# Moving the modulation loads of a two-block transformer kernel around its latent-projection stage

## The reference, cut to what matters

```
mod = silu(c) @ w_ada + b_ada                 # one vector of 12288; c is one row, w_ada is 2048 x 12288
sh1, sc1, gt1, sh2, sc2, gt2 = split(mod, 6)  # six vectors of 2048
h = rms_norm(x, g_norm1) * (1 + sc1) + sh1
q_d, k_d, v_d, cq, ckv, k_pe = split(h @ w_in)         # differential attention, and the latents
a_out = differential_attention(...)                    # 8 heads
q_m = rms_norm(cq) @ w_q_b ; kv = rms_norm(ckv) @ w_kv_b   # the latent projections
b_out = latent_attention(...)                          # 8 heads
x = x + gt1 * (concat(a_out, b_out) @ w_out)
h2 = rms_norm(x, g_norm2) * (1 + sc2) + sh2
x = x + gt2 * ((silu(h2 @ w_gate) * (h2 @ w_up)) @ w_down)
```

## Time and profile before

| | us |
|---|---|
| median of 3 runs (2666.29 to 2670.49) | 2669.9 |
| the profiled execution | 2669.1 |
| its span, first to last instruction | 2667.0 |
| TensorE busy | 2594.2 (97%) |
| VectorE busy | 1547.3 (58%) |
| ScalarE busy | 1164.6 (44%) |

### The profile page before, as it was taken

One profiled execution on the slowest core, in us unless ns is written; L12 is line 12 of the kernel. 1 busy time (PEld: TensorE's weight loads), 2 busy tenths in 40 slices (PEclk: granted clock), 3 DMA queues, 4 the chain that ended last, 5 costly groups with the idle time before them and its releaser, 6 DMA issues.

```text
span 2667.0 us, 32922 instructions
## 1 busy us (share of the span) xinstructions
PE 2594.2 (97%) x12142; PEld 2084.7 (78%) x12142; DVE 1547.3 (58%) x1700; ACT 1164.6 (44%) x1522; POOL 53.9 (2%) x86
## 2 busy tenths in 40 slices
PE   6999989899999999999999999999999999999997
PEld 2667757688888888887888888888888888888886
DVE  1456754567776555557655454556555555555555
ACT  2344554343434444443544455444444444444443
POOL 1010110000000000000000000000000000000000
PEclk8999989999999999999999999999999999999999
DMA  9967776657777655555655545566565555555652
GB/s 391 381 232 288 261 252 220 223 171 244 243 244 245 192 190 189 189 190 189 206 189 189 174 158 166 196 201 226 188 200 189 190 188 189 189 189 188 190 188 100
DMA packets 262881, 561.72 MB, mean 211 GB/s; under 512 B 9250, under 2 KB 13556, under 8 KB 261900
## 3 DMA queue, kind: packets, MB, share of 16 engines
q1 hardware_dynamic: 260688, 549.25, 61.2%
q0 software_dynamic: 1728, 9.19, 1.0%
q10 hardware_dynamic: 380, 2.13, 0.2%
HBM read 556.32 MB, written 4.21 MB: 210 GB/s over the span
## 4 chain that ended last, share of the span: by engine, by line
PE 83%; DVE 2%; ACT 1%; issue 1%; DMA 0%; POOL 0%; DVEq 0%; POOLq 0%; ACTq 0%
PE acc L633 78%; PE bank L716 2%; PE bank L663 1%; DVE w_lo L1678 0%; PE acc L857 0%; PE acc L909 0%; PE acc L855 0%; PE bank L728 0%; PE bank L866 0%; DMA raw<-in_w_ada 0%; PE bank L690 0%; DVE wide L2194 0%; DVE x_res L2198 0%; PE acc L1068 0%; PE acc L1069 0%
## 5 line engine op out<-in xcount | busy, mean ns | idle before, releaser
L1678 DVE TENSOR_TENSOR w_lo<-raw,w_hi 128x1024 fp32r<-128x1024 f32 x852 | 1037.7, 1224 | 827.5 <-ACT w_hi L1154 798.6
L1154 ACT ACTIVATE w_hi<-raw 128x1024 fp32r<-128x1024 f32 x852 | 901.0, 1060 | 1065.1 <-PE acc L633 953.8
L633 PE MATMUL acc<-w_hi,actT_hi 128*128 128x512 f32 (+1 forms) x2112 | 833.6, 395 | 1.2 <-DVE actT_lo L1813 0.8
L633 PE MATMUL acc<-w_hi,actT_lo 128*128 128x512 f32 (+1 forms) x2112 | 821.2, 389 | 0.0
L633 PE MATMUL acc<-w_lo,actT_hi 128*128 128x512 f32 (+1 forms) x2112 | 820.8, 389 | 0.0
L633 PE MATMUL acc<-w_hi,mixT_hi 128*128 128x512 f32 (+1 forms) x1280 | 504.3, 394 | 9.1 <-DVE mixT_lo L1803 4.3
L633 PE MATMUL acc<-w_hi,mixT_lo 128*128 128x512 f32 (+1 forms) x1280 | 498.0, 389 | 0.0
L633 PE MATMUL acc<-w_lo,mixT_hi 128*128 128x512 f32 (+1 forms) x1280 | 497.6, 389 | 0.0
L633 PEld LDWEIGHTS acc<-w_hi,actT_hi 128*128 128x128 f32 x2112 | 397.3, 188 | 106.5 <-issue 21.9
L633 PEld LDWEIGHTS acc<-w_hi,actT_lo 128*128 128x128 f32 x2112 | 397.1, 188 | 83.0
L633 PEld LDWEIGHTS acc<-w_lo,actT_hi 128*128 128x128 f32 x2112 | 397.7, 188 | 79.3 <-issue 1.2
(11 more groups left out here) (272 smaller groups left out, 1049.1 us busy)
## 6 DMA issues: line engine op xcount, KB each, us to landing
raw<-in_w_ff SPq DMA_DIRECT2D x128, 1024.0 KB, 5.1
raw<-in_w_in SPq DMA_DIRECT2D x108, 1024.0 KB, 5.2
raw<-in_w_ada SPq DMA_DIRECT2D x64, 1024.0 KB, 5.2
raw<-in_w_gate SPq DMA_DIRECT2D x44, 1024.0 KB, 5.1
raw<-in_w_up SPq DMA_DIRECT2D x44, 1024.0 KB, 5.2
raw<-in_w_down SPq DMA_DIRECT2D x44, 1024.0 KB, 5.1
early_mix<-in_w_ada SPq DMA_DIRECT2D x16, 1024.0 KB, 9.5
wide<-in_w_ada SPq DMA_DIRECT2D x16, 1024.0 KB, 8.8
```

The costliest lines, as they stand in the source:

```text
L633: last_mm = pe.matmul(acc[p][:, t, 0:width], act[x][:, k0 + c, t * P:(t + 1) * P], w[:, u % SPL, c * NW:c * NW + width], start=first and c ...
L1154: act.activation(w_hi[:, u % SPL, :], raw[:, ld % RAW, (u % DU) * 1024:(u % DU + 1) * 1024], ACT.Copy) \
L1678: dve.tensor_tensor(w_lo[:, u % SPL, :], raw[:, ld % RAW, (u % DU) * 1024:(u % DU + 1) * 1024], w_hi[:, u % SPL, :].bitcast(F32), ALU.subt ...
```

## The change

It does five things.

1. The 24 pairs of a loads stand elsewhere. Before: behind w loads 13, 15, 16, 18, 20, 21, 23, 24, 26, 28, 29, 31, 33, 34, 36, 37, 39, 41, 42, 44, 46, 47, 49, 50. After: behind 12 to 14, 16 to 18, 20 to 22, 24 to 26, 28 to 30, and then 38 to 40, 42 to 44, 46 to 48. None is left behind w loads 31 to 37.
2. The rows of gt1 and gt2 are made from `part` directly: a product with ones (gt2) or with the selector `sel` (gt1) sums over the partitions and spreads at once. The columns of gt1 and gt2 and their biases in `cols2` are gone; a row takes two banks.
3. The biases of gt1 and gt2 are loaded into `grow` by GpSimd (1 MB each), and VectorE adds the sums to them.
4. VectorE makes `w_lo` of unit 0 before the columns of group 1, and that of unit 1 after `modulated(0)`.
5. The part of a load 17 moves from the prologue to behind unit 0.

```diff
+PAIRS_AT = [12 + i for i in range(19) if i % 4 != 3] + [38 + i for i in range(13) if i % 4 != 3][:9]
+GAPS = [2 * (i in PAIRS_AT) for i in range(54)]
-GAPS = [0] * 12 + [2 * ((i + 1) * 24 // 39 - i * 24 // 39) for i in range(39)] + [0] * 3
...
-    return steps + [("part", LEAD), ("part", LEAD + 1)]
+    return steps + [("part", LEAD)]
...
-        return [LEAD + 1 + v] if 0 < v < NPRO - LEAD - 1 else []
-    events = [("row", n) for a in products(u - 3) for n in completed(a) if n >= len(GROUPS)]
-    events += [("columns", n) for a in products(u - 2) for n in completed(a)]
+        return [LEAD + 1 + v] if 0 <= v < NPRO - LEAD - 1 else []
+    events = [("row" if n >= len(PROLOGUE) + 4 else "columns", n) for a in products(u - 2) for n in completed(a)]
...
 # TensorE
-            def part_row(n_, kind=GT2, g=0):
-                pe.wait_ge(mod_ready, L.value("groups", n_ + 1))
-                b, _ = wait_bank()
-                for j in range(4):
-                    col = mcol[:, kind, 4 * g + j:4 * g + j + 1]
-                    ins = pe.matmul(bank[b][:, j * P:(j + 1) * P], col.broadcast_to([P, P]), ident, start=True,
-                                    stop=True)
-                ins.then_inc(bank_full[b], 1)
+            def part_row(n_):
+                pe.wait_ge(part_ready, L.value("groups", sums_of(n_), 4))
+                for j in range(2):
+                    b, _ = wait_bank()
+                    if n_ < len(GROUPS):
+                        pe.matmul(bank[b][:, :], sel[:, j:j + 1].broadcast_to([P, P]), part[:, :], start=True,
+                                  stop=True).then_inc(bank_full[b], 1)
+                    else:
+                        pe.matmul(bank[b][:, 0:S], ones[:, :], part[:, j * S:(j + 1) * S], start=True,
+                                  stop=True).then_inc(bank_full[b], 1)
...
 # GpSimd
             pool.wait_ge(o_ready, H)
+            pool.dma_start(grow, b_ada("gt1").partition_broadcast(P)).then_inc(gt1_bias, 16)
             pool.dma_start(bf[:, :], A["b_f_2"][0, :].partition_broadcast(P)).then_inc(bf_in, 16)
...
             inv_rms(D, TT)
+            pool.wait_ge(xg_ready, 4)
+            pool.dma_start(grow, b_ada("gt2").partition_broadcast(P)).then_inc(gt2_bias, 16)
...
 # VectorE
+            def part_row(n_):
+                for j in range(2):
+                    b = next_bank()
+                    if n_ < len(GROUPS):
+                        dve.wait_ge(gt1_bias, 16)
+                        at_ = (2 * (n_ - len(PROLOGUE) - 4) + j) * NW
+                        dst, sums = grow[:, at_:at_ + NW], bank[b][:, :]
+                    else:
+                        dve.wait_ge(gt2_bias, 16)
+                        dst, sums = grow[:, bass.ds(j * S if L.i is None else L.i * NW + j * S, S)], bank[b][:, 0:S]
+                    link(dve.tensor_tensor(dst, sums, dst, ALU.add))
                     dve.sem_inc(bank_free[b], 1)
...
             for s in prologue():
+                if s == ("columns", 1):
+                    split()
                 if s[0] in todo_of:
                     todo_of[s[0]](*s[1:])
-            for _ in range(DU):
-                split()
             modulated(0)
-            for _ in range(AHEAD - DU):
+            for _ in range(AHEAD - 1):
                 split()
```

More of the change, by code:

```diff
@@ L44 @@
                                ("sh2", 16))),
-                      (ROWS2, (("sc2", 16), ("gt1", 16), ("gt2", 16), ("gmix", 16), ("gmlp", 16), ("convw", 24),
+                      (ROWS2, (("sc2", 16), ("gmix", 16), ("gmlp", 16), ("convw", 24),
                                ("gq", 1), ("gk", 1), ("gqn", 1), ("gkn", 1)))):
@@ L151, in banks_of @@
 def banks_of(u):
-    return len([1 for e in modulation(u) if takes_bank(*e)])
+    return sum(2 if what == "row" else 1 for what, n_ in modulation(u) if takes_bank(what, n_))
 def pieces_of(n_):
@@ L352, in build @@
         gt_in = sem("gt_in")
+        gt1_bias = sem("gt1_bias")
+        gt2_bias = sem("gt2_bias")
         gt_used = sem("gt_used")
@@ L682, in part_columns @@
                 ins.then_inc(bank_full[b], 1)
-            def part_row(n_, kind=GT2, g=0):
-                pe.wait_ge(mod_ready, L.value("groups", n_ + 1))
-                b, _ = wait_bank()
-                for j in range(4):
-                    col = mcol[:, kind, 4 * g + j:4 * g + j + 1]
-                    ins = pe.matmul(bank[b][:, j * P:(j + 1) * P], col.broadcast_to([P, P]), ident, start=True,
-                                    stop=True)
-                ins.then_inc(bank_full[b], 1)
-            def gt1_row(g):
-                part_row(GROUPS.index((PARTS.index("gt1"), 8 * (g // 2), 8)), PARTS.index("gt1"), g)
+            def part_row(n_):
[8 more added lines that the diff above has]
+                                  stop=True).then_inc(bank_full[b], 1)
             stages = {}
@@ L927, in _ @@
             for g in range(4):
[L928 to L931, removed]
+                at = {j: lambda j=j: run(heads_at(16 + j)) for j in range(3)} if g == 0 else None
                 group(g % 2, MIXT, 8, k0=8, at=at, ready=(lambda j: outputs_taken(H + UC * j)) if g == 0 else None)
@@ L1410, in _ @@
                 if g == 0:
-                    at = {0: lambda: run(heads_at(16)), 1: lambda: [run(heads_at(17)), skip_banks(1)],
-                          2: lambda: run(heads_at(18))}
+                    at = {j: lambda j=j: run(heads_at(16 + j)) for j in range(3)}
                 else:
-                    at = {0: lambda g=g: group_sums(g - 1), 1: lambda: skip_banks(1)}
+                    at = {0: lambda g=g: group_sums(g - 1)}
                 units(4, at)
@@ L1612, in _ @@
             b_ada = lambda name: A["b_ada"][0, PARTS.index(name) * D:(PARTS.index(name) + 1) * D]
-            for name, src in (("sc2", b_ada("sc2")), ("gt1", b_ada("gt1")), ("gt2", b_ada("gt2")),
-                              ("gmix", A["g_mix_2"][0, :]), ("gmlp", A["g_mlp_2"][0, :]),
+            for name, src in (("sc2", b_ada("sc2")), ("gmix", A["g_mix_2"][0, :]), ("gmlp", A["g_mlp_2"][0, :]),
                               ("convw", A["conv_w_2"][0, :, :].rearrange("j n -> (j n)"))):
@@ L1739, in part_columns @@
                 b = next_bank()
[L1740 to L1749, removed]
-                    else:
-                        link(dve.tensor_tensor(dst, sums, bias, ALU.add))
+                kind, k0, width = GROUPS[n_]
@@ new lines, in part_columns @@
+                name = PARTS[kind]
+                cols, rows_ = (cols1, ROWS1) if name in ROWS1 else (cols2, ROWS2)
+                at_ = lambda base: slice(base + k0, base + k0 + width)
+                dst, sums, bias = mcol[:, kind, at_(0)], bank[b][:, 0:width], cols[:, at_(rows_[name][0])]
+                if width == 8:
+                    link(dve.tensor_tensor(dst.rearrange("p (h j) -> p h j", h=2),
+                                           sums.rearrange("p (j h) -> p h j", h=2),
+                                           bias.rearrange("p (h j) -> p h j", h=2), ALU.add))
+                else:
+                    link(dve.tensor_tensor(dst, sums, bias, ALU.add))
@@ new lines, in part_columns @@
+                dve.sem_inc(bank_free[b], 1)
+                if name in ("sc1", "sc2"):
+                    link(dve.scalar_tensor_tensor(out=dst, in0=dst, scalar=1.0,
+                                                  in1=cols1[:, at_(ROWS1["g" + name[2]][0])], op0=ALU.add,
+                                                  op1=ALU.mult))
+                dve.sem_inc(mod_ready, 1)
+            def part_row(n_):
[5 more added lines that the diff above has]
+                        dst, sums = grow[:, at_:at_ + NW], bank[b][:, :]
+                    else:
+                        dve.wait_ge(gt2_bias, 16)
+                        dst, sums = grow[:, bass.ds(j * S if L.i is None else L.i * NW + j * S, S)], bank[b][:, 0:S]
+                    link(dve.tensor_tensor(dst, sums, dst, ALU.add))
@@ L1752, in part_columns @@
                     dve.sem_inc(bank_free[b], 1)
[L1753 to L1772, removed]
             def units(n, at=None):
@@ L2129, in _ @@
             for g in range(4):
[L2130 to L2134, removed]
+                units(4, {j: lambda j=j: run(heads_at(16 + j)) for j in range(3)} if g == 0 else None)
                 if g == 0:
```

## The result

The changed kernel took 2677.2 us (median of 9 runs, 2674.72 to 2686.7) against 2668.9 for the kernel before (9 runs). The ratio is 1.0037, 95% interval 1.0027 to 1.0046: slower by about 10 us, where 2.05 us faster (2667.9) was forecast and 2675 was the upper end of the range. The profiled execution took 2680.65 us, 3.5 above the median of the nine; its span is 2678.2 us, 11.2 more than before, so what its profile shows of waits is somewhat more than a median execution has.

The account below looks back on a forecast made before the run. TensorE, busy 97% of the span, was taken as the bound; 7.4 + 1.9 + 3.5 - 0.95 - 9 - 0.3 + 0.5 - 1.8 - 3.3 = -2.05 us gave 2667.9 us as median, range 2660 to 2675.

Parts of the forecast that it names:

- What the stage gives back: Latent projections, 304 to 349 us: without four pairs and a columns step, 9 us saved, at most 11.8.
- -0.3 and +0.5: 349 to 376 us: pair behind unit 72 gone, -0.3 us; new pair behind unit 74 replacing a columns step, +0.5 us.
- floor of 33.2 us: Stage from 304 to 349 us: VectorE's remaining work, under which the stage can't fall.
- weak end: Smallest gain of the stage, 5.8 us: 2.8 us where TensorE is full, plus one bank wait of 2.96 us.
- Their waits: Six more neighbouring pairs before the latent projections, second a loads late by 0.59 us each: +3.5 us, between 1.0 and 6.7.
- third rival: Triples pile up: a pair's sum holds a bank, 2.96 us in each of five triples, +14.8, 2682.7 us; chance 0.17.
- the rows: Rows of gt1 and gt2 by products with ones: columns steps go, -1.8 us and -3.3 us.
- the start: Unit 0 begins near 59.7 instead of 61.80 us, unit 1 stays near 65.8; taken as 0 (0.9 possible).
- `w_out`: Last pair stands behind unit 94, before the second half's neighbour wait: -0.95 us, 0 if the wait only moves.
- upper end: The sum of the terms at their slow ends, given as +8.0 us.
- the first rival: Stage gives back all: falls to 33.2 us, neighbours wait 0.16; sum -8.3 us, 2661.6 us; chance 0.30.
- the second (the start): Start is worth unit 0's gain, 2.1 us, if something other than that load holds unit 1: 2665.8 us; chance 0.10.

Follow-up runs that it names:

- e3: The kernel before with only the new places of the pairs; ratio 1.0042, 2678.0 us.
- e4: Changed kernel, but the first a load of each pair frees its ring slot when TensorE has read it; ratio 1.0023, 2672.8 us.
- e5: Changed kernel, but pairs behind the 11 old w loads up to 29, then behind 38 to 50 without a gap; ratio 1.0011, 2670.3 us.
- e1: Changed kernel with the 24 pairs back at their old places; ratio 0.9979, 2662.8 us.
- e2: Changed kernel with the start as before (a load 17 in the prologue, both splits before modulated(0)); ratio 1.0033, 2676.6 us.
- e7: Old places, rows and start as changed; pairs behind w loads 31 to 37 make one of four products per a load; ratio 0.9979, 2661.3 us.
- e8: Changed kernel with the exponentials of the differential heads one unit later; ratio 1.0022, 2674.0 us.

## Why the prediction was wrong

**What the stage gives back** is the step that failed. It said -9 us between 304 and 349, and -0.3 and +0.5 behind it, 8.8 in all. The profile after has -3.4 (from the start of unit 60 to that of unit 72) and +0.8, so 2.6; that of e3, with the same places, -4.8 and -0.3, so 5.2. Its premise was half right: the `w_q_b` loads did stop being late, and VectorE's sum did stop holding the bank, though other steps of VectorE held it, up to 2.4 us. The wrong half was to take VectorE's idle time for a result of the late loads, of which 2.3 us would stay of 8.8: 9.4 stayed. I had read who released each wait, but not asked what would be next: with the loads in time, ScalarE waited for VectorE's maxima instead (3.4 us before, 9.6 after), and `w_hi` behind it. The floor of 33.2 us was never near. Even the weak end, 5.8, counted TensorE's work as if the clock stayed, and the pair behind unit 74 took 3.64 us where 1.9 was counted.

**Their waits** was the second miss: +3.5 us forecast, with 6.7 as its end, 12 in the profile after and 8 in e3's. I had priced neighbours singly, from pairs with a gap in front of them. In a triple the third pair meets a ring that is already behind; the longest waits, 2.22 and 2.46 us, fell on third pairs of a triple (units 50 and 58). The reason given, the release, was a part of it (e4: 2.2 us less waiting than e3); the 2.22 us at unit 50 were one late part of a load. The sum had no term for a bank that comes late (1.5 us) nor for the clock that idle time costs (3.5 us). The third rival's threshold, 1.5 us a triple, was crossed at (12 - 3.5) / 5 = 1.7 in this profile, but not in e3's, (8.3 - 3.5) / 5 = 1.0; and what there was were late a loads and one bank wait, not five bank waits of 3 us. So "slower" came true, but not by this rival's mechanism. Alone this miss makes -2.05 + 8.5 = +6.5 us, the stage's alone -2.05 + 6.2 = +4.2, both +12.7; the profiles differ by 11.2, and the terms that came out a little better make up the rest.

**Right:** 1.85 us a pair where TensorE is full (from unit 60 to unit 61 the kernel before takes 4.86 us and e5, without a pair there, 3.01); the rows (5.6 measured at the old places, 5.1 forecast, though e1's interval allows 3 to 8); the start, where unit 0 came at 59.63 and unit 1 at 65.99, held by ScalarE's third `w_hi`; both bias loads hidden, with no wait of VectorE for either. `w_out` gave 2.3 where the terms said 1.8. The upper end adds up to 7.9, not 8.0.

One rule looked borne out and was not. The Trainium skill, DMA: Bandwidth & Descriptors, Specifications, puts one core's share of HBM at about 358 GB/s, which would have put up to 5 us on the triples. The trace after shows 401 GB/s over 63 us again, and e4 took out part of the triples' waits while moving more bytes per second. So the extra time was not a limit at 358, though it came in the same place.

**The cases:** the first rival (all given back) fell with e5 and with the stage's time in all six profiles with no pairs behind w loads 31 to 37, the second (the start) with unit 1's start at 65.99; e2 agrees.

**Open:** why taking four pairs and two columns steps out of the stage shortens it by only some 1 us, 3 at most. The lower clock takes part of it and the ring of waits the rest; no run separates them, and e7, which was meant to take TensorE's work alone away, did not take it away. Nor is it settled how much the rows save at the new places.

## What to carry to other kernels

Where each engine waits for another in turn, an engine's idle time need not shrink when filler leaves the stage: here that gained some 1 us, 3 at most, and the filler cost its full time, and waits besides, where it went. Nor is the idle time free room: two more pairs cost twice their own time, and busy times don't show where that begins. So move filler in both directions before judging. Before removing the cause of a wait, ask which wait comes next behind it. In a ring of buffers ask who gives the slot free and what is queued before it there; a release by the reader instead of by a later store gained 4 us where pairs stood close, barely above the noise. And when an experiment leaves work out, look in its trace whether the time went too: in e7 it had not.

## What was not expected of the hardware

Four products that each use a quarter of the array run side by side, so one of them alone takes as long as all four: a pair took 1.90 us with a quarter of its products and 1.92 with all.

With filler gone and more idle time between TensorE's instructions (7.6 us in 41.7, against 6.1 in 43.2), its granted clock was lower, 0.88 instead of 0.96 and 0.81 instead of 0.87, so that 7.8 us less work by the forecast's prices shortened its busy time by 2.8 us. In e4 and e5, with as little work, the clock was 0.92 and 0.82 and the busy time some 4.9 us less.

A 1 MB load can be ready but for one of its 16 parts: of the one issued at 269.43 us 15 had landed after 4.7 us and the last after 7.4. One part 2.3 to 3.0 us behind the others occurs in the profiles of the changed kernel, e1, e2 and e8, and it decides whether an execution has such a wait.
